# Output weight sums placed one step earlier, in buffers of the folds of x

## The reference

```
proj = rmsnorm(x, norm_g) @ w_in
y_a  = (dilated attention * silu(z_a)) @ w_pa
y_b  = (block attention  * silu(z_b)) @ w_pb
merged = sigmoid(r_a + b) * y_a + sigmoid(r_b + b) * y_b
out  = rmsnorm(x + merged @ w_out, final_g)
```

## Time and profile before

| what | us |
|---|---|
| median of 3 runs | 433.71 (433.39 to 433.98) |
| the profiled execution | 433.87 |
| its span, first to last instruction | 432.0 |
| PE busy | 421.3 |
| DVE busy | 298.3 |
| ACT busy | 228.1 |
| POOL busy | 218.8 |

### The profile page before, as it was taken

How to read it: one execution, slowest core, us unless ns; L and a number is a source line. 1 busy time by engine, 2 the same in 40 slices (tenths; PEclk the granted TensorE clock), 3 DMA queues, 4 the chain that set the end, 5 groups by cost and what they waited for, 6 DMA issues and landing times.

```text
span 432.0 us, 7151 instructions
## 1 busy us (share of the span) xinstructions
PE 421.3 (98%) x2557; PEld 375.6 (87%) x2557; DVE 298.3 (69%) x511; ACT 228.1 (53%) x475; POOL 218.8 (51%) x156
## 2 busy tenths in 40 slices
PE   7899999999999999999999999999999999999994
PEld 6789998899889988998888888888999999988883
DVE  3879745275578766657956774596687768589955
ACT  5745556356466765556645564454444545542633
POOL 4854432252276545474469456343435433734890
PEclk9999999999999999999999999999999999999998
DMA  8782244936899979221520326540443134199905
GB/s 279 246 253 99 99 139 121 279 80 246 309 273 388 363 244 307 99 99 49 148 97 2 98 91 239 196 132 3 134 135 103 48 121 134 39 411 407 394 5 195
DMA packets 48835, 76.70 MB, mean 178 GB/s; under 512 B 4360, under 2 KB 39200, under 8 KB 47264
## 3 DMA queue, kind: packets, MB, share of 16 engines
q1 hardware_dynamic: 43904, 67.38, 47.0%
q10 hardware_dynamic: 4896, 8.86, 5.5%
HBM read 55.21 MB, written 14.73 MB: 162 GB/s over the span
## 4 chain that ended last, share of the span: by engine, by line
PE 94%; DMA 1%; ACT 1%; DVE 1%; issue 1%; SPq 0%; DVEq 0%; ACTq 0%
PE ps L1130 15%; PE ps L1131 15%; PE ps L1134 15%; PE ps L1330 5%; PE ps L1329 5%; PE ps L1328 5%; PE ps L1171 4%; PE ps L1173 4%; PE ps L1172 4%; PE ps L1237 4%; PE ps L1218 3%; PE ps L1266 3%; PE ps L1375 3%; PE ps L1376 3%; PE ps L1377 3%; PE ps L1256 2%
## 5 line engine op out<-in xcount | busy, mean ns | idle before, releaser
L950 POOL TENSOR_TENSOR w_lo<-raw,w_hi 128x1024 fp32r<-128x1024 f32 x39 | 96.4, 2474 | 104.2 <-ACT w_hi L1429 104.1
L1130 PE MATMUL ps<-hT_hi,w_hi 128*128 128x512 f32 x240 | 97.7, 407 | 1.1 <-DVE hT_lo L1823 1.1
L1134 PE MATMUL ps<-hT_lo,w_hi 128*128 128x512 f32 x240 | 93.8, 391 | 0.0
L1131 PE MATMUL ps<-hT_hi,w_lo 128*128 128x512 f32 x240 | 93.8, 391 | 0.0
L1022 POOL TENSOR_TENSOR w_lo<-raw,w_hi 128x512 fp32r<-128x512 f32 (+1 forms) x34 | 42.4, 1266 | 49.5 <-ACT w_hi L1451 49.5
L1134 PEld LDWEIGHTS ps<-hT_lo,w_hi 128*128 128x128 f32 x240 | 45.0, 188 | 9.9
L1130 PEld LDWEIGHTS ps<-hT_hi,w_hi 128*128 128x128 f32 x240 | 45.2, 188 | 7.4 <-issue 1.3
L1131 PEld LDWEIGHTS ps<-hT_hi,w_lo 128*128 128x128 f32 x240 | 45.3, 189 | 6.1
L1171 PE MATMUL ps<-w_hi,hT_hi 128*128 128x256 f32 x160 | 45.5, 285 | 0.0
L1173 PE MATMUL ps<-w_lo,hT_hi 128*128 128x256 f32 x160 | 44.7, 280 | 0.0
L1172 PE MATMUL ps<-w_hi,hT_lo 128*128 128x256 f32 x160 | 44.6, 279 | 0.0
(11 more groups left out here) (263 smaller groups left out, 1043.2 us busy)
## 6 DMA issues: line engine op xcount, KB each, us to landing
raw<-in_w_in SPq DMA_DIRECT2D x25, 1024.0 KB, 6.6
KTs<-KTs SPq DMA_DIRECT2D x20, 256.0 KB, 4.3
folds<-folded_early SPq DMA_DIRECT2D x4, 1024.0 KB, 8.8
wq_raw<-in_w_out SPq DMA_DIRECT2D x4, 1024.0 KB, 11.5
output_weight_sums<-ws_parts ACTq DMA_DIRECT2D x8, 512.0 KB, 6.7
folded<-folds SPq DMA_DIRECT2D x4, 1024.0 KB, 6.3
t_three<-output_weight_sums SPq DMA_DIRECT2D x2, 2048.0 KB, 11.4
raw<-in_w_out SPq DMA_DIRECT2D x3, 1024.0 KB, 5.0
```

Source lines behind the costliest of these rows:

```text
L950: nc.gpsimd.tensor_tensor(ring(w_lo, n, kt), src, ring(w_hi, n, kt).bitcast(F32), ALU.subtract).then_inc(lo_ready, 1)
L1130: pe.matmul(out, wh, hh, start=(k == 0), stop=False)
L1131: pe.matmul(out, wl, hh, start=False, stop=False)
L1134: return pe.matmul(out, wh, hl, start=False, stop=(k == kts - 1))
```

## The change

Sums 0 to 5 move to places one step or half a step earlier: the first is begun in step 12, and (17, 0) falls out. The buffers are taken in another order: the first two sums go to the places of `fold_two` and `fold_one`, and ACT's casts wait for the folds that stood in their buffer. The store of fold 3 moves from behind load 10 to behind load 9 and the load of the first block of w_out. POOL's third sums move one slot down.

```diff
-FOLD_STORES = [7, 8, 9, 10]
-W_PLACES = [(13, 1), (14, 1), (15, 1), (16, 0), (16, 1), (17, 0), (17, 1), (18, 1), (19, 1), (20, 1), (21, 1), (22, 0)]
+FOLD_STORES = [7, 8, 9, 9]
+W_PLACES = [(12, 1), (13, 1), (14, 1), (15, 1), (16, 0), (16, 1), (17, 1), (18, 1), (19, 1), (20, 1), (21, 1), (22, 0)]
...
-THIRD_SLOTS = [15, 17, 19, 21]
+THIRD_SLOTS = [14, 16, 18, 20]
...
             b = j % NWB
-            return ws_parts[:, b, :, :] if b < 3 else (ws_fourth if b == 3 else ws_fifth)[:, :, :]
+            return ws_parts[:, b - 2, :, :] if b > 1 else (ws_fifth if b else ws_fourth)[:, :, :]
...
                 if n in W_LOADS:
                     load_output_weights(W_LOADS.index(n))
+                if n == FOLD_STORES[3]:
+                    store_fold(3)
...
             def ws_high(j):
 
-                if j < NWB:
-                    act.wait_ge(folds_out[2], 16)
-                    act.wait_ge(folds_out[3], 16)
-                else:
+                if j == 0:
+                    act.wait_ge(folded_lo, 4)
+                elif 2 <= j < NWB:
+                    act.wait_ge(folds_out[2 + (j == 4)], 16)
+                elif j >= NWB:
                     act.wait_ge(ws_out[j % NWB], 16 * (j // NWB))
```

## The result

The changed kernel takes 434.93 us (434.82 to 435.15, 8 runs) against 433.69 (433.39 to 433.98, 8 runs): 1.24 us more, ratio 1.0028, 95% interval 1.0018 to 1.0038. Forecast were 435.2 and slower. The profiled execution took 434.93 us, span 433.1.

The account below looks back on a forecast made before the run. The prediction took PE, busy without a break, to bound the kernel; 0 for what goes, 0 for what moves and +1.5 us for one wait gave 433.71 + 1.5 = 435.2 us, range 433.9 to 437.1.

Parts of the forecast that it names:

- What bounds: PE, busy without a break in steps 12 to 22: work off other engines gains 0, new PE waits count in full.
- What costs: End of step 12: DVE waits for the first w_out block with head 5 behind it, delaying ACT's copy; 1.5 us.
- Its size: Step 14: PE's weight load for head 4's values waits from 108.62 to 110.12, taken as 1.5 us.
- Three terms: Steps 12 to 14: block's landing 11.5 us after issue, sum 0 on DVE 0.81, release to first product 0.25.
- From where it decides: First w_out block's landing: if in by 103.3, PE sees no wait and the time stays 433.7 us.
- the shared queue: Rival on SP: fold 3's store delays the first w_out block by up to 3.1 us, 438.3 us; chance 0.08.
- the felt stall: Rival in step 14 or 15: ACT's 6.3 us stall held PE, so 1.3 us come back, 432.4; chance 0.05.
- In time: Rival: the first w_out block lands early enough that PE hardly waits, 433.7 to 434.5 us; chance 0.17.

Follow-up runs that it names:

- e1: Changed kernel with the twelve places of the weight sums as they were before the change: 433.72 us against 433.68 for the kernel before, ratio 0.9999.
- e3: Changed kernel with the first w_out block loaded behind load 8 in place of load 9: 433.59 us, ratio 1.0002 to the kernel before.
- e6: Changed kernel with ACT's copy of head 4's turned probabilities ahead of head 5's exponentials in step 13: 433.57 us, ratio 1.0000 to the kernel before.
- e2: Changed kernel with the store of fold 3 behind load 10 again, as before the change: 435.04 us, ratio 1.0037 to the kernel before.
- e7: Changed kernel with GpSimd's third sums in their old slots 15, 17, 19 and 21: 435.09 us, ratio 1.0041 to the kernel before.
- e5: Changed kernel with the first w_out block issued ahead of the store of fold 2, second in its queue: 433.36 us, ratio 0.9993 to the kernel before.
- e4: Changed kernel with the first w_out block issued behind the store of fold 3, fourth in its queue: 437.81 us, ratio 1.0107 to the kernel before.
- e8: Changed kernel with the first w_out block loaded behind load 10 in place of load 9: 443.38 us, ratio 1.0240 to the kernel before.

## Why the prediction was right

- *What bounds:* PE without a break, so that a wait on it is paid in full and a wait off it is free. Held: 6.33 us off ACT were worth 0 (e1), 1.3 us on PE some 1.3.
- *What costs:* sum 0 in DVE's order ahead of head 5. Held in place, in path and in kind (e1, e3, e6).
- *Its size:* 1.5 was forecast; PE's loss in the profile is about 1.5, and the medians differ by 1.24 (1.36 and 1.41 in e2 and e7, which have the same wait). Three terms were a little off and nearly made up for each other, which is luck. The block took 11.81 us and not 11.5. Head 5's mask began 0.60 us behind the sum's start (104.73 to 105.33) and not 0.81: the sum took 0.70, and the mask began 0.10 before its end. From ACT's release to the product it took 0.06 us (109.86 to 109.92), not 0.25, which I had from the start of the kernel.
- *From where it decides:* a block in by 103.3 was to be free. By the measured delay of 5.2 us and a product due at 108.85 it is 103.6. No run has a landing near that point: e5's, with a sum at 101.05, was free, the changed kernel's, at 104.73, was not, and e4's cost its delay in full.
- *Rivals:* the shared queue is out (e2), the felt stall is out (e1). "In time" did not occur in the profiles with the store in either place, but is what e5 brings about.
- *What was left out:* ACT's own wait of 3.31 us at the cast of sum 0 was only implied, and no rival had PE's clock in it.

No version beats both kernels: e3, e5 and e6 are as fast as before and not measurably faster, for PE has nothing more to give there.

## What to carry to other kernels

On an engine that runs in program order, an early place for a piece of side work is only free if its data are there: put the wait behind the work that others need, not ahead of it. When the bound engine has no gaps, price a change by the covers that it eats, follow each late instruction to what stands behind it in every queue, and look for the copy that is held up without needing anything of what it waits behind. Time won off the bound engine is not won.

## What the runs showed of the hardware that was not expected

PE's clock fell once soon after a short wait. In the profile of e2, PE's wait of 1.4 us ended at 110.34, and from 111.4 on the granted clock stood at 0.50, 1.2 GHz, for 3.4 us (stretches of e2, busy us of PE, PEld, DVE, ACT, POOL, then granted clock, DMA share, GB/s):

```profile
105.00:110.40 5.40, 4.02 (x27) 3.29 (x25) 5.09 (x11) 2.82 (x11) 0.02 (x1) 1.00 0.69 176
111.40:114.80 3.40, 3.40 (x12) 2.72 (x12) 1.84 (x4) 2.34 (x10) 2.61 (x2) 0.50 1.00 418
115.00:120.00 5.00, 5.00 (x29) 4.31 (x27) 2.93 (x6) 2.92 (x5) 1.49 (x2) 1.00 0.77 289
```

PE had been busy 4.02 of the 5.40 us up to 110.4, and all of the time from there to 111.4. Matmuls at half speed for 3.4 us lose 1.7, an estimate; this execution took 436.9 us where the other five of its kernel took 434.6 to 435.2. In the profiles of the changed kernel, of e7 with the same kind of wait and of e4 with two, the clock stayed at 1.00 behind it. That the wait brings the clock down is not shown. Of the 22 runs of the changed kernel, e2 and e7 two have a mean granted clock of 0.994 or less (e2's profiled one, 0.993, and the 437.72 us of e7, 0.988); but so have 7 of 99 runs of the kernels without this wait (before, e1, e3, e5, e6), at 0.992 to 0.994 and 0.8 to 1.4 us over their medians. Where the clock fell in those 7, no profile tells.

In e8 the lower clock came during the wait of 7.25 us and lasted until 117.1:

```profile
105.00:110.30 5.30, 1.53 (x11) 1.05 (x9) 0.00 (x0) 0.00 (x0) 0.00 (x0) 1.00 0.90 316
110.40:117.10 6.70, 3.32 (x10) 2.67 (x10) 4.77 (x10) 2.51 (x10) 0.00 (x0) 0.50 0.54 213
117.20:124.00 6.80, 6.80 (x38) 5.73 (x38) 4.72 (x10) 5.09 (x15) 3.65 (x2) 1.00 0.29 114
```

There it was free: PE went through the matmuls before the product of values at half speed, and the second wait, 1.47 us in e4, was not seen, since ACT's copy, which ended at 117.30, was the later of the two all the same. Of the other runs of e8, those at 445.0 and 443.1 us have a lower mean granted clock than the profiled one, 0.981 and 0.987 against 0.990, so the lower clock lasted longer in them, wherever it fell. The runs at 444.5 and 443.4 have 0.990 as well; why they took longer stays open.
